# Recurrent stage as running products of gates, with the table copies spread over other chunks

## What is computed

```python
f = lb + (1 - lb) * sigmoid(z)          # gate, per token and channel
log_f, k = log(f), 1 - f
# S_t = diag(f_t) S_{t-1} + k_t^T v_t,   o_t = q_t S_t      (4 heads, 128 x 128 states)
b = cumsum(log_f, axis=time)            # inside a chunk
decay = exp(where(causal, b[t] - b[s], -inf))
A = einsum('td,sd,tsd->ts', q, k, decay)
o = A @ v + (q * exp(b)) @ S
S = exp(b_last) * S + (k * exp(b_last - b)).T @ v
```

## Time and profile before

| what | us |
|---|---|
| median of 3 runs (3430.22 to 3447.2) | 3441.47 |
| span of the profiled execution | 3439.0 |
| PE busy in it | 2775.5 |
| DVE busy in it | 2075.3 |
| ACT busy in it | 1222.6 |
| POOL busy in it | 803.0 |
| DMA moved | 848.12 MB |
| stage of the recurrence (388.4 to 558.1) | 169.7 |
| first gather issued at | 686.96 |
| gathers of full rate, about 790 to 2005 | 1215 |

### The profile page before, as it was taken

One profiled execution on the slowest core, in us unless ns is written; L12 is line 12 of the kernel. 1 busy time (PEld: TensorE's weight loads), 2 busy tenths in 40 slices (PEclk: granted clock), 3 DMA queues, 4 the chain that ended last, 5 costly groups with the idle time before them and its releaser, 6 DMA issues. The chain is left out here.

```text
span 3439.0 us, 38992 instructions
## 1 busy us (share of the span) xinstructions
PE 2775.5 (81%) x14561; PEld 2306.7 (67%) x14561; DVE 2075.3 (60%) x3720; ACT 1222.6 (36%) x2191; POOL 803.0 (23%) x724
## 2 busy tenths in 40 slices
PE   6999888995565565565666679989999999899998
PEld 5887677785455555455555667667888777778886
DVE  3224686587776854784455545357875465678753
ACT  2112433245555555555556531242220102422201
POOL 0002453124444444444444412001000000110000
PEclk9999999997777777767777879989999999999999
DMA  6999999789999999999999952202232231022222
GB/s 219 316 296 283 302 302 300 222 302 389 421 421 421 420 422 421 420 416 421 419 420 418 421 227 92 74 1 86 97 98 92 80 116 56 1 92 97 93 91 80
DMA packets 155057, 848.12 MB, mean 247 GB/s; under 512 B 15440, under 2 KB 15696, under 8 KB 88208
## 3 DMA queue, kind: packets, MB, share of 16 engines
q0 software_dynamic: 82624, 575.97, 41.5%
q1 hardware_dynamic: 72272, 269.99, 24.8%
HBM read 841.70 MB, written 136.31 MB: 284 GB/s over the span
## 5 line engine op out<-in xcount | busy, mean ns | idle before, releaser
L210 PE MATMUL PS<-AR_r,RHI 128*128 128x512 f32 (+2 forms) x1912 | 751.4, 393 | 27.4 <-DVE RING_r L1615 8.5
L909 PE MATMUL PS<-IDN,HL 128*128 128x128 f32 x2688 | 488.5, 353 | 331.0 <-ACT HL L1435 331.0
L212 PE MATMUL PS<-AR_r,RING_r 128*128 128x512 f32 (+2 forms) x1912 | 746.9, 391 | 0.0
L1821 DVE SCALAR_TENSOR_TENSOR AR<-AR 128x1024 f32<-128x1024 f32 x410 | 501.3, 1224 | 368.4 <-DMA AR<-peer_uv,XC 368.0
L909 PEld LDWEIGHTS PS<-IDN,HL 128*128 128x128 f32 x2688 | 423.0, 184 | 395.4 <-ACT HL L1435 388.4
L211 PE MATMUL PS<-AR_r,RHI 128*128 128x512 f32 (+1 forms) x1688 | 657.6, 390 | 0.0
L555 POOL DMA_INDIRECT AR<-peer_uv,XC x410 | 467.6, 1141 | 616.1 <-ACT HL L1435 315.1
L1613 DVE CAST RHI<-RING 128x1024 fp32r<-128x1024 f32 x256 | 178.7, 698 | 450.7 <-DMA RING<-in_wstream 448.1
L210 PEld LDWEIGHTS PS<-AR_r,RHI 128*128 128x128 f32 x1912 | 364.5, 191 | 107.7 <-issue 19.1
L212 PEld LDWEIGHTS PS<-AR_r,RING_r 128*128 128x128 f32 x1912 | 364.0, 190 | 74.1
L909 PE MATMUL PS<-IDN,AR 128*128 128x128 f32 x1408 | 255.4, 353 | 174.1 <-ACT AR L1435 174.1
(11 more groups left out here) (369 smaller groups left out, 3740.5 us busy)
## 6 DMA issues: line engine op xcount, KB each, us to landing
RING<-in_wstream SPq DMA_DIRECT2D x304, 512.0 KB, 3.5
peer_uv<-in_peer_u SPq DMA_DIRECT2D x50, 1024.0 KB, 17.1
peer_uv<-in_peer_v SPq DMA_DIRECT2D x50, 1024.0 KB, 17.7
peer_uv<-in_peer_u POOLq DMA_DIRECT2D x14, 1024.0 KB, 22.1
peer_uv<-in_peer_v POOLq DMA_DIRECT2D x14, 1024.0 KB, 23.0
AR<-peer_uv,XC POOLq DMA_INDIRECT x410, 14.5
XL<-in_xl SPq DMA_DIRECT2D x1, 2048.0 KB, 8.1
AR<-in_strips POOLq DMA_DIRECT2D x1, 2048.0 KB, 8.1
```

The lines of the kernel that those rows point to most:

```text
L210: pe.matmul(out, sh, mh, start=start, stop=False)
L212: return pe.matmul(out, sl, mh, start=False, stop=stop)
L909: mm = pe.matmul(sum_bank(tt, k), scaled_row(n)[:, P * k:P * k + P], IDN[:], start=(j == 0 and k % 4 == 0), stop=(j == SLOTS - 1), is_tran ...
L1821: dve.scalar_tensor_tensor(u, u, 1.0, HT[:, n // SLOTS, :], ALU.mult, ALU.mult, accum_out=RAW[:, n:n + 1]).then_inc(dotted, 1)
```

## The change

It does the recurrent stage for both directions in turn inside one stage, with products of gates:

- no logarithm, no sum in time, no exponential, no difference. `KS[d]` (k = 1 - f) is made by ACT; DVE makes `QE[d] = f * q`. Then levels 0 to 7: at each level, `grow_state` multiplies half of q and half of k by the gate product of the neighbouring block (two DVE products of 1024 elements each), and then the block's own product (1024, 512, ... 16 elements). POOL does the same for the context part (1024 of 3072 columns).
- PE computes at levels 0 to 5 only diagonal blocks of 32 x 32: 64 small matmuls (32 stationary, 32 moving columns) for each level and direction; level 6 has 32 of 32 x 32, level 7 has 16 of 64 x 64. They go in turn to four (two) groups of output partitions.
- DVE takes entries for levels 0 to 5 under a mask of 512 instead of 2 x 1024 elements; ACT copies them, and levels 6 and 7, into `AT`.
- modulation chunks go in pairs (two output groups in turn) instead of one by one: 4 ahead of level 0, then 2 behind each of the 12 level and direction steps of levels 0 to 5. The `keep_clock` matmuls of the stage are gone, and barrier 4 is passed without a wait.
- the lower bound on the gates ahead of barrier 2 (two DVE instructions, L1709) is gone; the mask conversion on POOL is four small copies behind its last bias.
- of the 128 copies SP issues 80, POOL 48. Counted by the place where they are queued:

| behind | before | after |
|---|---|---|
| chunks 16 to 47 (SP) | 48 | 48 |
| barrier 1, ahead of the projections (POOL) | 0 | 4 |
| chunks 48 to 51, still in the projections (SP) | 5 | 2 |
| neighbourhood attention (POOL) | 20 | 20 |
| chunks 52 to 79 (SP) | 35 | 14 |
| barrier 5, read-out (POOL) | 4 | 8 |
| chunks 80 to 87 (SP) | 8 | 8 |
| barrier 6, ahead of the output projection (POOL) | 0 | 8 |
| chunks 88 to 91 (SP) | 4 | 8 |
| split of chunk 90 (POOL) | 4 | 8 |

The diff, cut to its core:

```diff
-POOL_COPIES = NA_HEADS // 2 * NCB + 12
+POOL_COPIES = NA_HEADS // 2 * NCB + 32
...
-        _more = 2 if _c % 4 == 0 and _c < FIRST["out"] else int(_c < FIRST["wq"])
-        _more = 4 if _c == FIRST["wq"] + 3 else _more
+        _more = int(_c % 2 == 0) if _c < FIRST["out"] else 1 if _c < FIRST["wq"] else 2 if _c < FIRST["wq"] + 4 else 0
...
             pool.dma_start(BT, t["na_bias"]).then_inc(s_bt, 16)
+            for _ in range(4):
+                copy_rows(pool, next(late), uv_copied_late)
             barrier(pool, 2)
...
+            for d in range(2):
+                pool.wait_ge(hg["k"], d + 1)
+                for lv in range(1, LEVELS):
+                    steps.wait()
+                    _, _, ks, k_by, total, by = grow(d, lv, slice(2048, 3072))
+                    steps.done(pool.tensor_tensor(ks, ks, k_by, ALU.mult))
+                    steps.wait()
+                    ins = pool.tensor_tensor(total, total, by, ALU.mult)
...
-            for _ in range(4):
+            passing(pool, 4)
+            barrier(pool, 5)
+            for _ in range(8):
                 copy_rows(pool, next(late), uv_copied_late)
             barrier(pool, 6)
+            for _ in range(8):
+                copy_rows(pool, next(late), uv_copied_late)
             pool.dma_start(KEYS, t["keys"]).then_inc(s_keys, 16)
...
             def modulate(n):
-                for _ in range(n):
+                for _ in range(n // 2):
                     i = next(made)
-                    modulation(FIRST["mod2"], [i], 6 + i // 16)
+                    modulation(FIRST["mod2"], (i, next(made)), 6 + i // 16)
+            def level(lv, d):
+                ...
+                for u in range(16):
+                    for a, b, m in blocks:
+                        ...
+                        mm = pe.matmul(to[a:a + m, :], KS[d][:, P * u + a:P * u + a + m], q[:, P * u + b:P * u + b + m],
+                                       start=True, stop=True, skip_group_check=True)
+                mm.then_inc(hg["a"], 1)
+            modulate(4)
+            for lv in range(LEVELS):
+                for d in range(2):
+                    level(lv, d)
+                    if lv < LEVELS - 2:
+                        modulate(2)
...
+            def grow_state(d, lv):
+                qs, q_by, ks, k_by, total, by = grow(d, lv, slice(0, 2048))
+                dve.wait_ge(hg["a"], 2 * lv + d + 1)
+                steps.wait()
+                dve.tensor_tensor(qs, qs, q_by, ALU.mult)
+                dve.tensor_tensor(ks, ks, k_by, ALU.mult).then_inc(hg["grown"], 1)
+                if lv < NEAR_LEVELS:
+                    take(d, lv)
+                dve.wait_ge(hg["grown"], 2 * (lv - 1) + d + 1)
+                steps.done(dve.tensor_tensor(total, total, by, ALU.mult))
```

More of the change, by code:

```diff
@@ L498, in _ @@
             pool.wait_ge(s_hm, 16)
-            pool.tensor_copy(HM, XCF).then_inc(masks_ready, 1)
+            full = XCF.rearrange("p (d l x) -> p d l x", d=2, l=LEVELS)
+            near = HM.rearrange("p (d l x) -> p d l x", d=2, l=NEAR_LEVELS)
+            pool.wait_ge(na["bias"], 2 * NA_STEPS)
+            for g in range(4):
+                r = slice(32 * g, 32 * g + 32)
+                pool.tensor_copy(near[r], full[r, :, 0:NEAR_LEVELS, r]).then_inc(masks_ready, 1)
+                pool.wait_ge(masks_ready, g + 1)
             pool.memset(MROWS[2], 0.0).then_inc(phase, 1)
@@ L851, in _ @@
+            passing(pe, 4)
+            barrier(pe, 5)
             for h in range(HG_HEADS):
@@ L1385, in _ @@
-                if d == 0:
-                    act.activation(EW, Z[1], ACT.Ln).then_inc(s["lf"], 1)
-                barrier(act, 4 + d)
+                act.activation(KS[d], Z[d], ACT.Identity, scale=-1.0, bias=par("one")).then_inc(hg["k"], 1)
+            whole = [x.rearrange("p (u t) -> p u t", u=16) for x in AT]
+            for d in range(2):
+                act.wait_ge(hg["zero"], d + 3)
+                act.wait_ge(hg["near"], 2 * (NEAR_LEVELS - 1) + d + 1)
+                for g in range(4):
+                    r = slice(32 * g, 32 * g + 32)
+                    ins = act.activation(whole[d][r, :, r], NEAR[d].rearrange("p (u t) -> p u t", u=16)[r], ACT.Copy)
+                ins.then_inc(hg["block"], 1)
@@ new lines, in _ @@
+            for d in range(2):
+                act.wait_ge(hg["a"], 2 * (LEVELS - 2) + d + 1)
+                for a in (0, 64):
+                    lo, hi = slice(a, a + 32), slice(a + 32, a + 64)
+                    r, c = (lo, hi) if d == 0 else (hi, lo)
+                    ins = act.activation(whole[d][r, :, c],
+                                         bank(2 * d + (LEVELS - 2) % 2).rearrange("p (u t) -> p u t", u=16)[r], ACT.Copy)
+                ins.then_inc(hg["block"], 1)
+            for d in range(2):
+                act.wait_ge(hg["a"], 2 * (LEVELS - 1) + d + 1)
+                r, c = HALVES if d == 0 else HALVES[::-1]
+                for x in range(2):
+                    ins = act.activation(whole[d][r, 8 * x:8 * x + 8, c],
+                                         bank(4 + x).rearrange("p (u t) -> p u t", u=8)[r], ACT.Copy)
+                ins.then_inc(hg["block"], 1)
@@ L1389, in _ @@
+            for d in range(2):
+                act.wait_ge(hg["totals"], d + 1)
+                for n, b in enumerate(HG_BLOCKS):
+                    act.wait_ge(hg["kt"], 6 * d + n + 1)
+                    act.activation(Z[d][:, 512 * b:512 * b + 512], bank(2 * d + n % 2), ACT.Copy).then_inc(hg["kz"], 1)
+            passing(act, 4)
+            barrier(act, 5)
             for h in range(HG_HEADS):
@@ L1706, in _ @@
                                                      LB[:, c:c + 1], ALU.mult, ALU.add))
-            steps.wait()
-            for d in range(2):
-                dve.tensor_scalar(Z[d], Z[d], LN_MIN, None, ALU.max)
             barrier(dve, 2)
@@ new lines, in take, with totals @@
+            def take(d, lv):
+                if lv >= 1:
+                    dve.wait_ge(hg["near"], 2 * (lv - 1) + d + 1)
+                mask = near[:, d, lv].unsqueeze(1).to_broadcast([P, 16, 32])
+                to, src = (x.rearrange("p (u t) -> p u t", u=16) for x in (NEAR[d], bank(2 * d + lv % 2)))
+                dve.copy_predicated(to, mask, src).then_inc(hg["near"], 1)
+            def totals(d):
+                dve.wait_ge(hg["context"], d + 1)
+                steps.wait()
+                dve.tensor_copy(EB[d].unsqueeze(2), Z[d].rearrange("p (u s) -> p u s", u=24)[:, :, P - 1:P]
+                                ).then_inc(hg["totals"], 1)
@@ L1774, in _ @@
+            for lv in range(LEVELS):
+                for d in range(2):
+                    if lv == 0:
+                        dve.wait_ge(hg["zero"], d + 1)
+                        dve.wait_ge(hg["a"], d + 1)
+                        take(d, lv)
+                    else:
+                        grow_state(d, lv)
+                    if lv == LEVELS - 1:
+                        totals(d)
+            for d in range(2):
+                dve.wait_ge(hg["totals"], 2)
                 for j in range(5):
-                    after(dve, s, "u", j + 1, 5)
```

208 lines of the change are left out of this document (68 added, 140 removed).

## The result

The kernel after takes 3459.1 us in the median, the kernel before 3440.6, measured beside it, 20 runs each: a ratio of 1.0055, interval 1.0046 to 1.0064, or 18.4 us. The forecast was 3455. Of the three terms of its sum, one came out within 2 us (+38), the other two were 4 and 8 us too favourable.

A forecast was written before the change was run, and what follows sets the result against it. The prediction took full DMA engines to bound the kernel, the change only shifting the first gather. Projections +13, recurrent stage -38 and the part behind it +38 gave +13, so 3455 us, range 3425 to 3495.

The forecast's parts named there:

- The frame: Up to the first gather: the change only shifts that moment, released by indices or last copy; nothing differs behind it.
- Part 1: Projections: four POOL copies issued ahead share the DMA engines and delay chunk 22, +13 us, bounds 0 and 16.
- PE doesn't see that: Attention: three copies fewer behind chunks 48 to 51 take 10 us off the backlog, without effect on PE.
- Part 2: Recurrent stage: 132 us instead of 169.7, so -38, bounds 118 and 160.
- The tail: End of the recurrent stage, without chunks: levels 6 and 7, transposes, states, last barrier and slower clock, together 41 us.
- The phase with chunks: Recurrent stage, levels 0 to 5: 12 periods of 6.8 us plus start and friction, 91 us.
- PE's level: Levels 0 to 5: 128 records at 0.035 us, 4.7 us a level and direction (3.4 to 7.0).
- Part 3: Recurrence to first gather: 40 copies remain, 49.3 MB at 295 GB/s take 167 us instead of 129, +38.
- PE binds the new stage: Rival: dearer records or a slower clock make the recurrent stage 156 us, +24 more, 3479; chance 0.25.
- Copies hidden: Rival: deep queues keep 330 GB/s, behind the recurrence 150 us, first gather at 677, -10, 3432; chance 0.15.
- early copies free: Rival: the early copies ahead of the projections cost nothing, no +13, so +0, 3442; chance 0.12.
- The sum: First gather: 388.4 + 13 + 132 + 167 = 700.4 against 687.0, +13.

The follow-up runs named there:

- e1: Kernel after with POOL's four early copies moved to SP, one more behind each of chunks 48 to 51: 1.0016 of the kernel before.
- e6: Kernel after with the 14 copies behind chunks 52 to 79 moved behind barrier 5: one run, 3491.3 us.
- e8: Kernel after with early copies moved behind chunks 48 to 51, blocks of 64 x 64, and eight POOL copies in the recurrent stage's tail: 3437.1 us, 0.9982.
- e3: Kernel before with the copies distributed as in the kernel after, old recurrence kept: 1.0142 of the kernel before.
- e2: Kernel after with the copies distributed as in the kernel before, so the new recurrence alone: 1.0018 of the kernel before.

## Why the prediction was right, point by point

**The frame held.** The first gather is the moment that counts, and in the kernel after the copies release it, not the indices. Over the runs of the table the first gather ranges from 671 to 778, and the time follows it: 3423.5 at 671, 3440.6 at 687, 3459.1 at 713, 3488.3 at 737, 3525.6 at 778. From the first gather to the end the 14 profiled executions take 2740 to 2755 us, so a difference of a few us in one of them can't be put down to the part ahead of it. A slip in the reading of the earlier trace rows changed nothing: the eighth and ninth slices stand at 7 and 8 tenths, not at 9 (they hold the output projection with its 0.63).

**Part 1 (+13).** Measured +17 at the end of the attention, +15 as the mean of eight executions. Chunk 22 landed at 117.1, forecast 115, and PE's idles for the chunks 20 to 22 grew from 4.3 us in all (2.04 and 2.21) to 15.4 (4.71, 9.82 and 0.85). The size was right to 4 us. Wrong was "PE doesn't see that" of the backlog behind the attention: e1 shows that four more copies there cost 6 us at the first chunk of the recurrent stage. The Trainium skill's page "DMA: Bandwidth & Descriptors", section "Issuing engines are not separate DMA queues", says that the transfers of all issuing engines share the same 16 engines. The trace agrees: four copies on POOL's queue put off a chunk on SP's by 14.6 us (102.48 to 117.09).

**Part 2 (-38), measured -30.** The tail was forecast as 41 and took 39.5. The phase with chunks was forecast as 91 and took 100.0. The step that failed is PE's level: "64 small matmuls, 128 records", 0.035 us a record, 4.7 us. The records are far shorter. From the earlier trace rows I had put them at 0.025 or more, which was said to be a bound and wasn't one: in the timeline of the kernel after 122 of them run in 1.37 us at the full clock, 0.011 each:

```profile
408.45 1.37 PE L847 MATMUL PS<-AR 128*32 128x32 f32 x122
```

What takes the time is that 128 records are 256 instructions: each level calls for a packet, and each packet costs 2.3 us of idle (42.3 in 18). A level thus costs 1.4 to 2 us of work and more than that in idle (35.3 us in the 12 steps, 2.9 a step), together about the 4.7 of the forecast. My number for the level was near the truth by luck, since a wrong price per record stood in for a wait that I didn't know; and the sum lacked that this wait and the chunks' come one after the other: 7.8 a step instead of 6.8. The Trainium skill's page "TensorE: Matmul & The Clock Gate", section "Wait — 56ns, not 53.3ns?", which I had cited for a floor of about 25 ns between the starts of matmuls, doesn't fit these, which go to four output groups in turn: even at two records a matmul, 61 matmuls in 1.37 us start at most 22 ns apart, and their weight loads run beside them.

**Part 3 (+38), measured +39.5.** Its step, full engines until the copies are through, held in six kernels: 167.5 to 170.7 with 40 copies, against 128.4 with 20. The 167 us owe something to luck: instead of 49.3 MB at 295 GB/s the engines moved 52.0 MB at 309 (SP issued 17 chunks in that stretch, not 12), and the two errors cancel. The rate was 292 in the read-out and 315 behind it, between the bounds. POOL's last eight were issued at 669.6, 124.7 behind the stage, forecast 122.

**The rivals.** "PE binds the new stage" was half of what happened: PE's step did pass the 6.8 of the DMA, but neither by the record's price nor by the clock alone. The clock did fall, to 0.74 where it had been 0.97. It stood at its lower level (0.50) behind the wait of 7.66 us for the first chunk and at the upper one (1.00) behind the next wait, of 1.55 us:

```profile
417.40:420.90 3.50, 3.42 (x38) 3.40 (x39) 0.00 (x0) 0.00 (x0) 3.19 (x5) 0.50 1.03 370
424.30:425.90 1.60, 1.60 (x51) 1.60 (x46) 0.74 (x1) 0.00 (x0) 1.44 (x3) 1.00 1.04 328
```

A pair of chunks behind a long wait took 3.4 us instead of 1.94, and e6 showed 11 us of the stage to go with the clock; but in e8 such a pair takes the same 3.4, and there the bytes set the step. "Copies hidden" is refuted by the rest of 168.3 in e3 (150 by that rival), "early copies free" by e1.

**The sum** of 13 stands against 26 at the first gather of the profiled executions and 18.4 in the medians. The forecast's 3455 is so near the 3459 partly because the profiled pair shows more of a loss than the median pair does.

## What to carry to other kernels

Moving work off a stage doesn't pay while the engines that move bytes are full everywhere: ask first which stage has room (here the tail that the change itself made, at 0.23), and put the bytes there. Cutting matmuls into many small ones has a price that no busy time shows: count instructions, and if PE waits on "issue" every 127 matmul records, make them fewer rather than smaller: blocks twice as wide and half as many took the wait from 42.3 us to 3.1. And an engine that reports a barrier behind its own transfers may report it when they land; let it report first if nobody needs them.

## What the runs showed of the hardware

- PE's instructions come in packets of 16 KB (256 of them) through the DMA engines. In the old stage, at one packet in 19 us, PE never waits for one; in the new one with small blocks it idles 1.1 to 1.6 us a packet with no copies in the stage, 2.2 to 2.4 with 14, and 0.9 with 35, where its waits for chunks cover the rest. With blocks of 64 (12 packets) it idles 3.1 us in all.
- Such a wait ends 1.2 to 1.6 us after a packet is through (44 waits in three kernels). The next packet starts 1.3 to 1.5 us after PE goes on when the DMA engines are idle, 3.5 to 6.1 when they are full of chunks and copies (the kernel after), 5.3 to 7.8 in e2. That it stands behind their transfers follows from this; at which engine it does so isn't shown.
- A drain of POOL waited for the landing of the transfers that POOL had issued: PE waited 6.6 and 11.7 us for it at barrier 5 and went on 1.4 us after the last landing both times; it waited 1.4 (for DVE) when POOL reported first.
- Small matmuls (32 stationary, 32 moving columns, four output groups in turn) ran at 0.011 us a record at the full clock, so that in the new stage the wait for their instructions cost more than their work.
